# Memory rows' projection moved behind the products for recurrence inputs and output gates, in a two-block transformer kernel on one Trainium2 core

## The reference

```
(sq, sk, sv, dq, dk, dv, iq, ik, iw, hq, hf, hi, hg, g_sb, g_dsa, g_hg) = split(h @ w_in_l)
o = hgrn2(heads(hq), heads(hf), heads(hi), lb)            # hi: the recurrence's inputs
o = rms_norm(o, onorm) * silu(heads(hg))                  # hg: its output gates
...
kvm = rms_norm_2(mem, g_mem[l]) @ w_mem_kv[l]             # second block, the memory rows
km, vm = split(kvm)
```

## Time and profile before

| | |
|---|---|
| median of 3 runs | 1654.42 us (1651.62 to 1655.16) |
| profiled execution, its own time | 1654.43 us |
| its span, first to last instruction | 1652.7 us |
| PE busy | 1492.3 us, 90% of the span |
| DVE busy | 712.2 us, 43% |
| ACT busy | 314.4 us, 19% |
| mean granted clock of TensorE | 0.964 of full speed |

### The profile page before, as it was taken

The page is one execution under the profiler, slowest core; times in us unless marked ns, Lnnn a source line. Parts: engine busy times, 40 slices in busy tenths (PEclk is TensorE's granted clock), DMA queues, the critical chain, the costliest instruction groups (busy, mean ns, idle before and its releaser), DMA issues.

```text
span 1652.7 us, 19708 instructions
## 1 busy us (share of the span) xinstructions
PE 1492.3 (90%) x8232; PEld 964.0 (58%) x8232; DVE 712.2 (43%) x1403; ACT 314.4 (19%) x642; POOL 22.7 (1%) x41
## 2 busy tenths in 40 slices
PE   8999999999999999999999999999997556667667
PEld 5687899699545888897799444455542212212212
DVE  2657664466664656755457652344321000000001
ACT  2234422122001225330222002234400000000000
POOL 0000000000000000000000003100000000000000
PEclk9999999999999999999999999999999889877799
DMA  8547124454452642334445456554699999999997
GB/s 308 187 152 253 53 101 153 153 175 183 153 192 70 216 153 102 103 103 153 153 156 191 164 175 202 189 203 181 267 393 409 409 409 409 409 409 409 409 409 285
DMA packets 134666, 380.25 MB, mean 230 GB/s; under 512 B 6260, under 2 KB 16628, under 8 KB 134384
## 3 DMA queue, kind: packets, MB, share of 16 engines
q1 hardware_dynamic: 131696, 369.60, 59.6%
q0 software_dynamic: 2880, 9.36, 1.8%
HBM read 377.31 MB, written 5.73 MB: 232 GB/s over the span
## 4 chain that ended last, share of the span: by engine, by line
PE 73%; DMA 19%; SPq 4%; DVE 3%; issue 1%; ACT 0%; DVEq 0%; ACTq 0%
PE bank L1047 14%; PE bank L1333 12%; PE bank L1379 12%; DMA region<-in_w 12%; PE bank L1040 10%; DMA ring<-in_w 7%; PE bank L1157 4%; SPq L856 3%; PE bank L1131 2%; PE bank L1525 2%; PE bank L1425 2%; PE bank L1274 2%; PE bank L1304 1%; PE bank L1306 1%; PE bank L1083 1%; PE bank L1107 1%
## 5 line engine op out<-in xcount | busy, mean ns | idle before, releaser
L1040 PE MATMUL bank<-hT,ring 128*128 128x256 f32 x832 | 186.7, 381 | 0.0
L1040 PEld LDWEIGHTS bank<-hT,ring 128*128 128x128 f32 x832 | 155.5, 190 | 24.1 <-issue 3.4
L1379 PE MATMUL bank<-region 128*128 128x512 f32 x320 | 140.6, 592 | 0.0
L1525 PE MATMUL bank<-region 128*32 128x512 f32 x640 | 91.2, 699 | 50.3 <-DMA region<-in_w 50.3
L1047 PE MATMUL bank<-ring,region 128*128 128x512 f32 (+2 forms) x352 | 128.0, 521 | 2.7 <-ACT region L1634 1.4
L1047 PE MATMUL bank<-ring,hT 128*128 128x512 f32 x256 | 113.0, 594 | 0.0
L1379 PEld LDWEIGHTS bank<-region 128*128 128x128 f32 x320 | 60.5, 190 | 74.6 <-issue 74.6
L1333 PE MATMUL bank<-region 128*128 128x128 f32 x768 | 100.5, 275 | 0.0
L1047 PEld LDWEIGHTS bank<-ring,region 128*128 128x128 f32 x352 | 62.4, 193 | 62.6 <-issue 52.5
L1333 PEld LDWEIGHTS bank<-region 128*128 128x128 f32 x768 | 93.0, 192 | 0.0
L1525 PEld LDWEIGHTS bank<-region 128*32 128x32 f32 x640 | 18.7, 118 | 118.1 <-DMA region<-in_w 80.0
(11 more groups left out here) (411 smaller groups left out, 2197.6 us busy)
## 6 DMA issues: line engine op xcount, KB each, us to landing
region<-in_w SPq DMA_DIRECT2D x48, 2048.0 KB, 23.9
ring<-in_w SPq DMA_DIRECT2D x31, 2048.0 KB, 23.8
ring<-in_w_in SPq DMA_DIRECT2D x27, 2048.0 KB, 8.2
ring<-in_w_up SPq DMA_DIRECT2D x16, 2048.0 KB, 8.3
ring<-in_w_down SPq DMA_DIRECT2D x32, 1024.0 KB, 6.0
own_slot<-in_w SPq DMA_DIRECT2D x8, 2048.0 KB, 23.8
ring<-in_w_out SPq DMA_DIRECT2D x6, 2048.0 KB, 9.0
ring<-in_w_in SPq DMA_DIRECT2D x6, 1536.0 KB, 6.9
```

The costliest lines, as they stand in the source:

```text
L1040: t = mm(b[:, 0:T], w[:, k, :], act[:, k, :], start=(k == 0), stop=(k == KD - 1))
L1379: t = mm(b[:, :], left[:, t2, :], right[:, t2, :], start=(c4 == 0 and t2 == 0), stop=(c4 == 7 and t2 == 1))
L1525: t = mm(b[32 * e:32 * e + 32, :], xg[:, 2 * c + k, 32 * e:32 * e + 32], w[e][:, 512 * k:512 * k + 512], start=(c == 0 and k == 0), stop=( ...
```

## The change

`kv` stands behind `hg` in `PROJ`, so its load and its products come after those of `hi` and `hg`. The turns of the memory rows keep their place (they are now ahead of the `hh` products). The broadcast `rsb` goes to the place ahead of `kv` in layer 0 and ahead of `sv` in layer 1. ACT copies `kv` out behind the copies of `hv` and the sigmoids of `hg`. DVE makes the weights' sums for `hh` right behind the corners of `iq`, in both layers. The order of the `give` calls follows PE's order.

```
-PROJ = (("d", 512, 2), ("iq", 512, 2), ("ik", 72, 2), ("kv", 512, 2), ("hi", 256, 2), ("hg", 256, 2), ("sv", 384, 2),
+PROJ = (("d", 512, 2), ("iq", 512, 2), ("ik", 72, 2), ("hi", 256, 2), ("hg", 256, 2), ("kv", 512, 2), ("sv", 384, 2),
...
             for n, _, w in projections(l)[1:-4]:
-                if n == "hi":
+                if n == ("sv" if l else "kv"):
                     bk.give((l, "rsb"))
-                if n == "kv":
+                if n == "hi" and l == 0:
                     give_turns(2, "memT", 0)
                     give_turns(2, "memT", 1)
...
-                    if name == "hi":
+                    if name == ("sv" if l else "kv"):
                         pe.wait_ge(consts_loaded, 32)
...
-                    if name == "kv":
+                    if name == "hi" and l == 0:
                         turn_half(N_MEM, 0)
                         turn_half(N_MEM, 1)
+                    if name == "kv":
                         turned(N_MEM, 0)
                         turned(N_MEM, 1)
...
                 for i in range(NT):
                     A_(hsg[i], four[:, 1, i, :], ACT.Sigmoid, scale=r_[i]).then_inc(sig_ready, 1)
+                if l == 0:
+                    act.wait_ge(rs_ready, N_MEM + 1)
+                    for i in range(NT):
+                        free(A_(mem_kv[:, i, :], read((0, "kv", i))[:, :], ACT.Copy, scale=rs[:, N_MEM, i:i + 1]),
+                             (0, "kv", i))
...
                 row_corner_sums(l, "iq")
+                quarter_sums_of_rows(l, "hh")
                 if l == 0:
                     norm(N_MEM)
...
                 V.tensor_reduce(ss14, sq14, AX.X, ALU.add).then_inc(head_sums, 1)
-                quarter_sums_of_rows(l, "hh")
```

More of the change, by code:

```diff
@@ L1713, in _ @@
                     norm(N_MEM)
[L1714 to L1717, removed]
                 act.wait_ge(head_sums, l + 1)
```

## The result

The changed kernel took 1667.07 us (median of 4 runs, 1665.25 to 1667.65) against 1654.47 us for the kernel before (4 runs, 1651.62 to 1655.16): ratio 1.0079, 95% interval 1.0067 to 1.0091. It is slower, by 12.6 us; 1668.1 had been forecast. Its profiled execution spans 1664.8 us.

A forecast was written before the change was run, and what follows sets the result against it. PE was taken to bound the kernel, with 73% of the chain of waits. Layer 0 +6.8, layer 1 +3.5 and clock +1.96 and +1.44 made 13.7 over 1654.4: 1668.1 us, range 1662 to 1671.5.

The forecast's parts named there:

- Bounds and path: Both layers: PE carries 73% of the chain of waits, so a delay of PE moves all that follows by as much.
- The gain ahead of `kv`: Layer 0: PE's 1.29 us wait ahead of `kv` is hidden by `hh`; 1.5 us gained if nothing else waited.
- Are `hi` and `hg` there?: Layer 0, `hh` products: weights there by 36.4, DVE's sums run 38.1 to 42.8, so PE has no wait.
- The bank in layer 0: Second tile of `kv` waits for DVE to free `ty0` of `hh`: PE idle 8.3 us, `hf` starts 6.8 us later.
- Layer 1: Second tile of `sv` waits for `ty0` of `hh`: PE idle 4.6 us, `hf` later, +3.5 us.
- The clock: After both gaps PE runs slower at a lower granted clock: 1.96 us in layer 0, 1.44 in layer 1.
- the borrowed rows: Earlier trace: first 8 records of 128x512 took +1.96 us, 16 experts' records +1.44 after idling; used as the clock's price.
- The sum: Whole kernel: 6.8 + 3.5 + 1.96 + 1.44 = 13.7 us on 1654.4, giving 1668.1 us.
- Rival 1: Both layers: the waits come but the clock does not fall; 1664.7 us, chance 0.20.
- Rival 2: Layer 0: `hf`'s load lands late, in 11.8 us, 3.7 more; 1671.8 us, chance 0.08.
- Rival 4: Downstream of the layers: the delay is swallowed by later waits; within 3 us of 1654.4, chance 0.05.
- Rival 3: Both layers: `ty0`'s bank is free in time, so not slower; 2.7 us gained, 1651.7 us, chance 0.05.

The follow-up runs named there:

- e1: Changed kernel with spare banks outside the rotation for the tiles that met a bank of `hh`, their turns skipped: 1654.75 us against 1652.81 before, ratio 1.0009.
- e2: Changed kernel with DVE taking the corners of `hh` ahead of the weights' sums for `hf`: 1649.92 us against 1652.81 before, ratio 0.9985.
- e7: Like e1, spare banks in the changed kernel, but the turns not taken are counted, so later tiles keep their banks: 1650.63 us against 1653.11 before, ratio 0.9985.
- e8: Layer 0 as in e2; layer 1 as in the kernel before, with only DVE's sums for `hh` moved early: 1652.20 us against 1653.11 before, ratio 0.9988.
- e9: The kernel of e2 run once more, on the same chip as e8: 1650.62 us against 1653.11 before, ratio 0.9986.
- e4_layer1: The change's PE and DVE orders in layer 1 only, layer 0 as in the kernel before: 1657.99 us against 1652.81 before, ratio 1.0032.
- e3: The change's PE and DVE orders in layer 0 only, layer 1 as in the kernel before: 1660.73 us against 1652.81 before, ratio 1.0050.

## Why the prediction was right

**Bounds and path.** Right. The two layers lose 13.4 us, and PE is 14.30 us later at the router (0.92 of it from the start) and 14.49 later among the last products of the experts (1652.79 against 1638.30).

**The gain ahead of `kv`.** Predicted 1.5 us; e1, e2, e7, e8 and e9, which have no wait behind it, show 1.52.

**Are `hi` and `hg` there?** Yes: DVE starts the sums at 38.90, 0.34 behind the start of the last corner of `iq`, without a wait.

**The bank in layer 0.** The wait is at the tile, from the instruction and for the reason that were named. Its size was put too high: the second tile of `kv` starts 70.65 - (56.16 + 6.87) = 7.6 us after it could have, and 8.3 was predicted. Of the 0.7, 0.3 is the load (7.8 for 8.1), and 0.3 the step from DVE's free to PE's start, which I took as 0.35 from the earlier trace rows, a row that says "issue" and not what it stands for; the rows of the changed kernel show 70.65 - (69.91 + 0.69) = 0.05, and 0.06 in layer 1.

**Layer 1.** By the same reckoning the wait is 576.61 - (567.17 + 5.16) = 4.3 against 4.6. What is gained beside it was 1.35 (4.28 + 1.79 - 4.72), 1.2 predicted. Two waits go, the one of 0.40 us at the third product of `hf` and one of 0.46 at the third product of `hh`, which the prediction left out without naming it when it took the length of `hh` from layer 0. With each the lost overlap of the two groups goes too, some 0.2 us. The row of the second, in the kernel before:

```profile
549.55 1.97 PE L1131 MATMUL bank<-own_slot,region 128*128 128x256 f32 x8 [0.46 <-DVE own_slot L2081]
```

**The clock.** This term was too low. Layer 0: 19.79 for the 48 records against 17.19 at full clock (24.06 for all 64 in e2, less 6.87), 2.60 us, for 1.96 predicted. Layer 1: 6.95 against 5.16, 1.79 for 1.44. The upper bound given for layer 0 was 2.9. In both layers the loss is close to half of the time in which products ran at the lower level: about 5.0 us in layer 0 (70.65 to 75.6), about 3.4 in layer 1 (577.5 to 580.9). That is what the borrowed rows could not give. The experts' group of the earlier trace rows ended at 1288.8, before its grant rose at about 1289.1, so it shows only what a group of its length can lose. And the first row, the source of the 1.96, is not shown to be a matter of the grant at all. In the kernel before, the profile has the grant at 1.00 while those 8 records run slowly, two to a window of 1 us and then four:

```profile
10.00:11.00 1.00, 1.00 (x2) 0.44 (x2) 0.00 (x0) 0.00 (x0) 1.00 (x3) 1.00 1.06 389
13.00:14.00 1.00, 1.00 (x4) 0.41 (x3) 0.00 (x0) 0.00 (x0) 0.00 (x0) 1.00 1.12 418
```

What slowed them stays open. The same 8 records took 6.34 us in the profile of the changed kernel and 6.63 in that of e7, so the borrowed price depended on which run was profiled; that it came within 0.7 us of the measured one is partly luck.

**The sum.** Layer 0: 7.62 - 1.52 + 2.60 = 8.70 (8.76 predicted). Layer 1: 4.72 (4.94). The wait's error and the clock's have opposite signs and nearly cancel, so the total of 13.4 against 13.7 flatters the single terms. The medians give 12.6, with an interval of 11.1 to 15.1 us by the ratio.

**Rivals 1, 2 and 4** did not come: the grant fell behind both gaps, the load landed in 7.8, and PE's delay was not given back. Rival 3 came only once DVE's order was changed, in e2.

## What to carry to other kernels

When steps are moved, write down for each bank or slot who held it one rotation earlier and what frees it; a moved step can put a slow releaser where a quick one stood, and then everything in that releaser's queue is on the path. Before accepting the loss, look whether the releaser can be taken ahead of what stands before it: one exchange in DVE's order made +12.6 us into -2.9 (e2) and -2.5 (e9). A rotation is shared by the whole program: turns skipped in the two layers made a wait at the router, over 600 us after the last of them.

## What the runs showed of the hardware that I had not expected

The same wait of 4.11 us in the middle of `sv` cost 1.79 us of clock in the changed kernel and 7.89 - 5.16 = 2.73 in e4_layer1. In e4 the grant was at 0.50 before PE resumed at 567.1 and stayed there past 571:

```profile
566.00:567.00 1.00, 0.00 (x0) 0.00 (x0) 0.97 (x3) 0.00 (x0) 0.00 (x0) 0.50 1.05 369
...
571.00:572.00 1.00, 1.00 (x3) 0.56 (x2) 0.09 (x1) 0.04 (x1) 0.00 (x0) 0.50 0.00 0
```

In the changed kernel PE resumed at 576.6 at full clock, and the grant fell only then, behind the end of the gap, while products were running:

```profile
576.00:577.00 1.00, 0.40 (x1) 0.30 (x2) 1.00 (x3) 0.08 (x1) 0.00 (x0) 1.00 1.06 372
577.00:578.00 1.00, 1.00 (x4) 0.53 (x3) 0.96 (x2) 0.98 (x3) 0.00 (x0) 0.74 1.07 376
...
579.00:580.00 1.00, 1.00 (x3) 0.54 (x2) 0.85 (x2) 0.99 (x4) 0.00 (x0) 0.50 0.00 0
```

So the price of a gap is not a function of its length alone. In each of these cases it is close to half of the time that products ran at the lower level: about 5.3 us in e4 for 2.73, about 3.4 in the changed kernel for 1.79. What sets how much of the lower level falls on products was not tested, and one execution does not fix it.

Nor does it take a gap. In e2 (and in e3 and e9) the grant fell just ahead of the router, with no idle time of PE over 0.25 us near it, behind products of 128x36; the kernel before kept 1.00 there. The same ten records, before and then in e2, and a window of e2:

```profile
1192.07 4.54 PE L1436 MATMUL bank<-region 128*128 128x512 f32 x10
```

```profile
1189.71 6.23 PE L1437 MATMUL bank<-region 128*128 128x512 f32 x10
```

```profile
1191.00:1192.00 1.00, 1.00 (x2) 0.33 (x1) 0.86 (x6) 0.38 (x1) 0.00 (x0) 0.50 0.63 193
```

Some 1.1 of these 1.7 us fall where the kernel before waits 0.91 us for DVE. The rest is lost: from the turns to the router e2 gains 1.87 us, and its layers gain 2.46.
